# A two-block decoder network on one core: the order of the last dilated heads, projection b, the share copy and the gate sigmoids

## The reference, cut to what matters

```python
proj = h @ w_in[l]
dq, dk, dv, sq, sk, sv, gate_logits = split(proj)
y_a = dilated_attention(rope(dq), rope(dk), dv) @ w_proj_a[l]   # 3 groups x 4 heads of 64
y_b = stick_breaking_attention(sq, sk, sv) @ w_proj_b[l]
gates = sigmoid(gate_logits + b_gate[l])
mixed = gates[..., :1024] * y_a + gates[..., 1024:] * y_b
x = x + mixed @ w_out[l]
```

## Time and profile before

| | us |
|---|---|
| median of 3 runs | 1413.79 |
| lowest, highest | 1412.91, 1413.82 |
| the profiled execution, its own time | 1412.05 |
| its span | 1410.2 |
| TensorE busy in the span | 1379.9 |
| VectorE, ScalarE busy | 1012.3, 741.6 |
| mean granted TensorE clock, of full speed | 0.997 |

### The profile page before, as it was taken

The page is one execution under the profiler, slowest core; times in us unless marked ns, Lnnn a source line. Parts: engine busy times, 40 slices in busy tenths (PEclk is TensorE's granted clock), DMA queues, the critical chain, the costliest instruction groups (busy, mean ns, idle before and its releaser), DMA issues.

```text
span 1410.2 us, 20202 instructions
## 1 busy us (share of the span) xinstructions
PE 1379.9 (98%) x7868; PEld 1173.8 (83%) x7868; DVE 1012.3 (72%) x1525; ACT 741.6 (53%) x1138; POOL 84.0 (6%) x93
## 2 busy tenths in 40 slices
PE   8999899999999998999999999999999999999998
PEld 6899788888888987888888777888888878888886
DVE  5566579777764757877788677887667876886665
ACT  5564455455455554555555666554445664644443
POOL 0000001000000000211110101000000000000000
PEclk9999999999999999999999999999999999999999
DMA  9844355555555333666555523458776533365562
GB/s 303 239 141 150 120 179 180 182 201 185 179 194 190 125 120 120 214 204 212 191 181 184 173 90 117 138 166 230 204 215 189 166 116 102 109 209 179 191 197 90
DMA packets 154326, 242.31 MB, mean 172 GB/s; under 512 B 4540, under 2 KB 107084, under 8 KB 153967
## 3 DMA queue, kind: packets, MB, share of 16 engines
q1 hardware_dynamic: 150514, 227.23, 49.3%
q0 software_dynamic: 3712, 13.77, 3.7%
q10 hardware_dynamic: 4, 0.01, 0.0%
HBM read 239.03 MB, written 1.97 MB: 171 GB/s over the span
## 4 chain that ended last, share of the span: by engine, by line
PE 89%; DVE 4%; ACT 3%; DMA 2%; issue 1%; POOL 0%; SPq 0%; DVEq 0%; ACTq 0%; POOLq 0%
PE ps L976 19%; PE ps L942 16%; PE ps L949 16%; PE ps L946 16%; PE ps L979 10%; PE ps L1078 3%; DMA raw<-in_w_in 2%; PE ps L1132 2%; PE ps L1147 1%; PE ps L1166 1%; DVE wlo L2203 1%; ACT whi L1726 1%; PE ps L1016 1%; PE ps L1018 1%; PE ps L1017 1%
## 5 line engine op out<-in xcount | busy, mean ns | idle before, releaser
L2203 DVE TENSOR_TENSOR wlo<-raw,whi 128x1024 fp32r<-128x1024 f32 (+1 forms) x432 | 538.7, 1258 | 197.5 <-ACT whi L1726 196.9
L1726 ACT CAST whi<-raw 128x1024 fp32r<-128x1024 f32 (+1 forms) x432 | 446.4, 1042 | 270.3 <-PE ps L949 167.7
L976 PE MATMUL ps<-act,whi 128*128 128x512 f32 x1184 | 325.1, 395 | 1.2 <-DVE wlo L2203 0.9
L942 PE MATMUL ps<-whi,mhi 128*128 128x512 f32 (+2 forms) x688 | 236.7, 393 | 1.9 <-DVE mlo L2230 1.9
L949 PE MATMUL ps<-whi,mlo 128*128 128x512 f32 (+2 forms) x688 | 231.6, 386 | 0.0
L976 PEld LDWEIGHTS ps<-act,whi 128*128 128x128 f32 x1184 | 204.9, 189 | 31.8 <-DVE wlo L2203 1.6
L946 PE MATMUL ps<-wlo,mhi 128*128 128x512 f32 (+2 forms) x688 | 231.4, 385 | 0.0
L979 PEld LDWEIGHTS ps<-act,wlo 128*128 128x128 f32 x1184 | 182.7, 189 | 25.5
L979 PE MATMUL ps<-act,wlo 128*128 128x256 f32 x1184 | 189.5, 281 | 0.0
L942 PE MATMUL ps<-whi,act 128*128 128x256 f32 (+1 forms) x512 | 169.4, 331 | 0.4 <-DVE wlo L2203 0.3
L949 PE MATMUL ps<-whi,act 128*128 128x256 f32 (+1 forms) x512 | 165.5, 323 | 0.0
(11 more groups left out here) (288 smaller groups left out, 1464.4 us busy)
## 6 DMA issues: line engine op xcount, KB each, us to landing
raw<-in_mlp_w SPq DMA_DIRECT2D x64, 1024.0 KB, 5.3
raw<-in_w_up SPq DMA_DIRECT2D x44, 1024.0 KB, 5.2
raw<-in_w_in SPq DMA_DIRECT2D x39, 1024.0 KB, 5.2
raw<-in_w_down SPq DMA_DIRECT2D x22, 1024.0 KB, 4.8
raw<-in_ev_w_in SPq DMA_DIRECT2D x10, 1024.0 KB, 5.1
raw<-in_w_out SPq DMA_DIRECT2D x8, 1024.0 KB, 5.0
raw<-in_xa_wkv SPq DMA_DIRECT2D x4, 1024.0 KB, 5.2
raw<-in_ev_w_out SPq DMA_DIRECT2D x4, 1024.0 KB, 5.2
```

The source lines that it names most:

```text
L942: nc.tensor.matmul(o, hi[:, kx, rows_], wh[:, k, c0:c0 + w], start=first and h == 0 and k == 0 and (tt == 0 or at[1] == 0), stop=False)
L976: nc.tensor.matmul(both, wh[:, k, w], act2[:, kx].rearrange("p i n -> p (i n)"), start=kx == 0, stop=False)
L1726: nc.scalar.copy(whi[:, m % HL, 0:w], raw[:, n % RAW, h * w:h * w + w]).then_inc(hi_done, 1)
L2203: nc.vector.tensor_tensor(wlo[:, m % HL, 0:w], raw[:, n % RAW, h * w:h * w + w], whi[:, m % HL, 0:w].bitcast(F32), ALU.subtract).then_inc( ...
```

## The change

In all, for each of the two layers:

- TensorE does the value products of a pair ahead of the turning of the same step (steps 4, 6 and 8). The last unit, 7, is no longer turned by the loop in step 9 but in the middle of projection b's first half, which moves up from step 9 to step 8; the half's six matmuls of the second row tile follow it, and then the turning of the shares. Step 9 is empty. Projection b's second half stays in step 10, after the last value products.
- VectorE copies unit 7 (before: ScalarE), and copies the shares (before: ScalarE). It takes the reciprocals and does the last `gate_out` in step 8 ahead of the copy of unit 6; the two splits of steps 8 and 9 stand after the copies of units 6 and 7. The remainder of `attended` is formed before the first gate product of b.
- ScalarE has no copy of unit 7 and none of the shares; its sigmoids follow straight on the splits of the loop, and the split of half f0+20 moves behind the rounding of `attended`.

```diff
--- before.py
+++ after.py
@@ -61,7 +61,6 @@
 DIFF_OUTS = (21, 23)
 DIFF_SUMS = (23, 25)
 EVEN_TURNS = (33, 35)
-PB_AT = 1
 WIDE_LAG, PAIR_LAG = 2, 2
 BIG = 1e30
 SENTINEL = -3e38
@@ -180,7 +179,7 @@
         for g in range(8):
             plan.group(("qk1", l, g), "act" if g % 2 else "dve")
         for g in ("b", "a"):
-            plan.group(("y1", l, g), "split" if g == "b" else "act")
+            plan.group(("y1", l, g), "split" if g == "b" else "dve")
         plan.job(("pb", l), tall(a["w_proj_b"][l], 0, 2))
         plan.job(("pa", l), tall(a["w_proj_a"][l], 0, 2))
         for g in range(4):
@@ -573,7 +572,7 @@
         for k, us in stages:
             for i, d in enumerate(us):
                 if d["wide"]:
-                    eng = ("dve", "act")[i % 2]
+                    eng = ("dve", "act")[i % 2] if i < len(us) - 1 else "dve"
                 elif k[0] == "even":
                     eng = "act" if d["joint"] or d["qt"] else "dve"
                 else:
@@ -1202,11 +1201,11 @@
                     for i in range(n + WIDE_LAG + 1):
                         if i < n and i % 2 == 0:
                             scores(i)
-                        if WIDE_LAG <= i < n + WIDE_LAG:
-                            turn(i - WIDE_LAG)
                         j = i - WIDE_LAG - 2
                         if j >= 0 and j % 2 == 0:
                             values(j)
+                        if WIDE_LAG <= i < n + WIDE_LAG - 1:
+                            turn(i - WIDE_LAG)
                         if each:
                             each(i)
                     return
@@ -1340,12 +1339,14 @@
                 def between_heads(i):
                     if 8 + i < 2 * NGC:
                         gate_half(8 + i)
-                    h = i - len(units_of["dil", l]) - PB_AT
-                    if 0 <= h < 2:
+                    n = len(units_of["dil", l])
+                    if i in (n, n + 2):
+                        h = (i - n) // 2
                         if h == 0:
 
-                            pe.wait_ge(at_t, first_unit["dil", l] + len(units_of["dil", l]))
-                        half_chunk(plan.jobs["pb", l][0], h, mhi, mlo, 2, [[(0, 512, yb(tt, 0)), (512, 512, yb(tt, 1))] for tt in range(TT)], True, True)
+                            pe.wait_ge(at_t, first_unit["dil", l] + n)
+                        half_chunk(plan.jobs["pb", l][0], h, mhi, mlo, 2, [[(0, 512, yb(tt, 0)), (512, 512, yb(tt, 1))] for tt in range(TT)], True, True,
+                                   middle=(lambda: turn_head(n - 1)) if h == 0 else None)
                         if h == 0:
                             turn_shares()
                     if i == 1:
@@ -1353,6 +1354,7 @@
                         pe.wait_ge(grp_dve, plan.by_number[plan.groups["y1", l, "b"]][2])
 
 
+                _, turn_head, _ = attention_steps(("dil", l))
                 attention(("dil", l), between_heads)
                 pe.wait_ge(attended_lo, l + 1)
 
@@ -1882,13 +1884,12 @@
                 split_half(f0 + 11)
                 attention(("dil", l), each=lambda i: split_half(f0 + 10 + i))
 
-                take(("y1", l, "a"), shares)
                 act.wait_ge(gate_pre, 2 * NGC * (l + 1))
                 for c0 in (D, 0):
                     nc.scalar.activation(gates[:, :, c0:c0 + D], gates[:, :, c0:c0 + D], ACT.Sigmoid).then_inc(gate_done, 1)
-                split_half(f0 + 2 * NGC + 4)
                 act.wait_ge(o_ready, o_counts["dil", l])
                 nc.scalar.copy(blocks(mhi, 0), attended).then_inc(attended_hi, 1)
+                split_half(f0 + 2 * NGC + 4)
                 split_half(f0 + 2 * NGC + 5)
                 stream_hi("mix", l, mhi, gs=(0, 1))
                 split_half(f0 + 2 * NGC + 7)
@@ -2460,20 +2461,25 @@
 
                 def between(i, after=False):
 
-                    if after != (i >= len(units_of["dil", l])):
+                    n = len(units_of["dil", l])
+                    if i == n and not after:
+
+                        dve.wait_ge(at_e, first_unit["dil", l] + n)
+                        nc.vector.reciprocal(rden[:, :, 0:HG], den[:, :, 0:HG]).then_inc(share_ready, 1)
+                        gate_out(3 + i // 2)
+                    if after != (i >= n):
                         return
-                    if after and i == len(units_of["dil", l]) + 1:
-
-                        dve.wait_ge(at_e, first_unit["dil", l] + len(units_of["dil", l]))
-                        nc.vector.reciprocal(rden[:, :, 0:HG], den[:, :, 0:HG]).then_inc(share_ready, 1)
-                    if i % 2 == 0 and i:
+                    if 0 < i < n and i % 2 == 0:
                         gate_out(3 + i // 2)
                     split_half(f0 + 10 + i)
 
                 attention(("dil", l), between, lambda i: between(i, True))
 
+                key = ("y1", l, "a")
+                group_ready(dve, key)
+                nc.vector.tensor_copy(shares, group_bank(key)).then_inc(grp_dve, 1)
+                dve.wait_ge(grp_dve, plan.by_number[plan.groups[key]][2])
                 dve.wait_ge(at_o, first_unit["dil", l] + len(units_of["dil", l]))
-                dve.wait_ge(grp_act, plan.by_number[plan.groups["y1", l, "a"]][1])
                 nc.vector.tensor_tensor(attended, ps[:, 6, :], shares, ALU.mult).then_inc(o_ready, 2)
 
                 def gate_b(c, tt):
@@ -2492,10 +2498,10 @@
                         nc.vector.tensor_tensor(o, o, gates[:, tt, D + 512 * c:D + 512 * c + 512], ALU.add).then_inc(mixed, 1)
 
 
+                dve.wait_ge(attended_hi, l + 1)
+                nc.vector.tensor_tensor(blocks(mlo, 0), attended, blocks(mhi, 0).bitcast(F32), ALU.subtract).then_inc(attended_lo, 1)
                 dve.wait_ge(gate_done, 2 * l + 1)
                 gate_b(0, 0)
-                dve.wait_ge(attended_hi, l + 1)
-                nc.vector.tensor_tensor(blocks(mlo, 0), attended, blocks(mhi, 0).bitcast(F32), ALU.subtract).then_inc(attended_lo, 1)
                 n = gate_b(0, 1)
                 split_half(f0 + 2 * NGC + 4)
                 gate_b(1, 0)
```

## The result

| | before | changed |
|---|---|---|
| median of 4 runs beside each other, us | 1413.35 | 1398.62 |
| lowest, highest | 1411.17, 1413.82 | 1397.80, 1399.12 |
| profiled execution: own time, span | 1412.05, 1410.2 | 1397.80, 1396.0 |
| mean granted clock | 0.997 | 0.999 |

The ratio is 0.9898 (95% interval 0.9881 to 0.9915): 14.4 us faster, with 12.0 to 16.8 in the interval. The forecast was 1401.0, range 1399.2 to 1404.2. The direction and the mechanism came as forecast. The time lies 0.6 us under the range and 2.4 under the forecast: the rows give a gain of 14.4 where 12.8 was forecast, and the forecast started from 1413.79, the median of three of these four runs of before; the fourth took 1411.17.

A forecast was written before the change was run, and what follows sets the result against it. ScalarE's list was taken to end last before projection a, with TensorE waiting. An earlier start (4.7 us) and restored clock (1.7) make 6.4 a layer, 12.8 for two; 1413.79 - 12.8 = 1401.0, range 1399.2 to 1404.2 with rivals.

The forecast's parts named there:

- What bounds the stretch: Before projection a, ScalarE's list was said to end last, not TensorE's; waits there 7.0 us over two layers.
- The cover for the copy of unit 6: Projection b's first row tile, 1.39 us on TensorE, covers VectorE's copy: 1.2 us of waiting removed, 0.3 to spare.
- Unit 7, shares, ScalarE: With both copies on VectorE, sigmoids end at 153.8, share copy is hidden, remainder at 157.5, gated sum by 163.9.
- The rival in which VectorE becomes the bound: VectorE's list runs late by 0.5 to 1.2 us a layer, giving 1402.0 to 1403.4; chance 0.17.
- steps 4 and 6 "cost at nothing": Exchanging values and turning there moves nothing else: costed at nothing, up to 0.1 us gained or lost each.
- a price without a sign, 0.11: On TensorE, a switch from one kind of work to another was put at about 0.11 us.
- projection a, 1.7 a layer: Its 24 matmuls take 5.5 us instead of 7.22 as the clock stays up: gain 1.7 us a layer.
- The tail: From the last gate matmul at 147.68, projection a starts at 158.4 instead of 163.08: gain 4.7 us a layer.
- The sum: Over both layers: 4.7 + 1.7 = 6.4 us a layer, 12.8 for two.
- The clock rival: Short tail pieces with switches count as idleness, projection a stays slow: 2 x 1.7 us lost, 1404.4; chance 0.06.
- the wait did not just move: Rival: sigmoids can't start at 148.8, ScalarE's chain again delays projection a, only 2.4 us gained: 1411.4; chance 0.04.
- "slower": Rival: VectorE's late copy of unit 6 stalls TensorE inside projection b's first half and lowers the clock: 1417; chance 0.03.

The follow-up runs named there:

- e5_sigmoids_only: Kernel before with one line moved: ScalarE does the sigmoids ahead of the share copy; 1403.77 us beside 1412.56, ratio 0.9939.
- e3_shares_scalar: Changed kernel, but ScalarE copies the shares again, ahead of its sigmoids; 1406.42 us, ratio to the kernel before 0.9956.
- e8_unit7_scalar: Changed kernel, but ScalarE copies unit 7 again, ahead of its sigmoids; 1400.98 us, ratio to the kernel before 0.9915.
- e4_turn_ahead: Changed kernel, but unit 7 is turned ahead of projection b's first half instead of in its middle; 1401.24 us, ratio to before 0.9917.
- e1_order_back: Changed kernel, but in steps 4 and 6 the turning stands ahead of the value products again; 1398.77 us beside the changed kernel's 1398.62.
- e6_idle_two: Changed kernel with two added ScalarE copies ahead of the rounding of the attention output; 1409.43 us, ratio to the kernel before 0.9977.
- e7_idle_three: Changed kernel with three added ScalarE copies ahead of the rounding of the attention output; 1413.77 us, ratio to the kernel before 1.0008.

## Why the prediction was right in its mechanism and wrong in its size

**What bounds the stretch.** Right: ScalarE's list ended last. Taking the sigmoids out from behind the share copy alone gives 8.6 us (e5_sigmoids_only); putting the share copy or unit 7's copy back ahead of them costs 7.8 and 2.4 (e3_shares_scalar, e8_unit7_scalar).

**The cover for the copy of unit 6.** Right, 1.2 forecast: 1.14 waits return in e4_turn_ahead. Its price is a little more, 1.3 a layer, for the turning behind a wait lasts 0.85 instead of 0.66.

**Unit 7, shares, ScalarE.** Right in order and near in time: sigmoids until 153.6 (forecast 153.8), share copy hidden, remainder at 156.95 (157.5), gated sum at 162.67 (163.9). The rival in which VectorE becomes the bound did not come; its list has 0.3 to spare. One reason shows in its timeline: where it doesn't wait, an instruction mostly starts 0.04 to 0.09 before the one ahead of it has ended.

**The failed step: steps 4 and 6 "cost at nothing".** I wrote that the exchange there "moves nothing else", and allowed 0.1 each way. It gives 0.18 in each, 0.36 a layer. I knew the switches only as a price without a sign, 0.11, read from starts in the timeline. From end to end the same switch, from value products to matmuls with weights, costs 0.2: the first gate matmul takes 0.31 instead of 0.12, the first two of projection b's second half 0.66 (154.74) instead of 0.46 (149.40). With the turning between the two, that switch is gone from steps 4 and 6. e1_order_back brings it back and shows that it is the order; why a gate matmul follows value products later than it follows a turning was not tried.

**The mis-sized term: projection a, 1.7 a layer.** It is 7.38 - 5.45 = 1.93. I measured the old length to the start of the turning in the timeline (170.30), 0.16 before the end of the last matmul, but took the new start from the chain; the rest is in the rounding of 5.5 for 5.45. I also called all of it the clock's. By the table above, 7.38 is 5.45, a restart of 0.3 and 1.6 of slow clock.

**The tail.** 147.68 to 163.08 was 15.40; it is 147.13 to 157.69, 10.56. Forecast was 10.72; 0.16 more gained. The parts went both ways. The turning of unit 6 takes 0.81 behind the value products, not 0.66 as behind gate matmuls; but the turning of the shares takes 0.44, not 0.58, and the second row tile behind the turning of unit 7 takes 1.38 (151.46 to 152.84), so the switch of 0.11 put on it wasn't there.

**The sum.** 0.36 + 0.23 + 0.16 = 0.75 a layer above 6.4. By rows: from the scores of step 4 to the product with `w_out`, 43.43 before (128.87 to 172.30) and 36.25 now (128.73 to 164.98), 7.18. From there to layer 1's product it is 368.56 and 361.37, 7.19. Together 14.37, for which 12.8 stood; behind layer 1's product the changed kernel is 0.3 longer, which leaves the 14.1 of the rest. From 1413.79, 14.37 less would have been 1399.4, within the range. The range itself was not quite its own sum: its bounds and the 0.9 of scatter, added outright, give 1399.1 to 1403.5, where 1399.3 to 1403 stood. That changes nothing, since 1398.62 lies under all of them.

**The rest of the miss**, 0.8 of 2.4 us, is the scatter of the runs. The later runs, 7 to 19 at a time, put the kernel before at 1412.4 to 1412.7, not at 1413.79, and the changed one at 1398.6 to 1398.9. Why the kernel before scatters stays open. Its clocks and the table suggest the waits, since the clock's part of one wait is anything from nothing to 2.9; but the clock of single waits was seen only in profiled executions, and e6_idle_two, which waits 3.2 us in each layer, spreads over only 1.6 us in 10 runs.

**The clock rival**, in which the short pieces of the tail count as idleness and the clock falls, did not come: it is 1.00 through the whole tail, with 0.96 us of standing before the product with `w_out` behind it. It stayed at 1.00 behind the waits of 0.9 in e5_sigmoids_only and e8_unit7_scalar and of 1.2 in the kernel before (151 to 156 us) as well. The mode that the Trainium skill describes on its page "TensorE: Matmul & The Clock Gate", section "A second HAM failure mode: psum-queue depth-cycling", is therefore not seen here at waits of 0.9 to 1.2 us.

**The other two rivals.** The sigmoids started at once behind the splits (148.60 for the table load), so the wait did not just move. In "slower", the copy of unit 6 comes late; it ended at 150.4, in time. What a late start of projection a costs e7_idle_three shows: 5.1 us of standing in each layer bring the changed kernel to 1413.77, which can't be told from the kernel before.

## What to carry to other kernels

Ask of each wait not how long it is but which engine's list ends last in it, and take the work out of that list that nobody there waits for: here two sigmoids that stood behind a copy. A removed wait of TensorE is worth its length, 0.2 to 0.3 us of restart, and, for the ten waits of 2.5 to 5.1 us in the table, mostly some 1.6 us of slow clock, though once nothing and twice 2.8 or 2.9; trading one wait for three shorter ones gave its gain back here. And when a piece of work is exchanged with its neighbour, price the switches on both sides, from end to end as the chain counts them, and not from starts alone.

## What the runs showed that was not expected

- TensorE's restart cost 0.3 us even behind a wait of 0.1 (5.78 against 5.45 for 24 matmuls), in both layers of the one profile that has such a wait.
- A gate matmul behind value products took 0.31 us, behind a turning 0.12, so exchanging two pieces of TensorE's own work gained 0.18 us with no wait in sight.
- The clock fell behind a wait of 2.5 and of 5.1 us alike, for 1.6 to 1.8 us beyond the restart, but two waits of 3.5 and 3.4 in one execution cost 2.8 and nothing. The Trainium skill's page "TensorE: Matmul & The Clock Gate", Part 1, says that the number of slow matmuls at a kernel's start varies from run to run for the same kernel; the rows show the same within one execution, from one layer's wait to the next.
- The kernel before spread over 4.1 us in 7 runs, the changed one over 1.6 in 4, side by side. That the removed waits took the scatter with them is not shown: e6_idle_two has such waits and spreads over 1.6 in 10 runs, e7_idle_three over 2.1.
